# Full row gathers without a bounds check, and the last expert weights loaded in eight pieces

## The reference

```python
top_val, top_idx = lax.top_k(logits, TOP_K)          # 4 of 32 experts for each of 512 tokens
gate = jax.nn.softmax(top_val, axis=-1)
...
def expert_block(args):                              # 1024 -> 2048 -> 1024, all float32
    xb, e = args
    hc = xb @ w1[e] + b1[e]
    glu = jnp.minimum(hc[..., :D_FF], SWIGLU_LIMIT)
    lin = jnp.clip(hc[..., D_FF:], -SWIGLU_LIMIT, SWIGLU_LIMIT)
    act = glu * jax.nn.sigmoid(SWIGLU_ALPHA * glu) * (lin + 1.0)
    return act @ w2[e] + b2[e]
...
y_assign = yrows[row] * sorted_gate[:, None]
out = jax.ops.segment_sum(y_assign, sorted_tok, num_segments=T)
```

## Time and profile before

| | us |
|---|---|
| median of 3 runs (1811.76 to 1812.91) | 1812.0 |
| the profiled execution | 1812.0 |
| its span, first to last instruction | 1810.3 |
| PE busy | 1712.9 |
| DVE / ACT / POOL busy | 451.7 / 385.9 / 105.0 |

### The profile page before, as it was taken

The page is one execution under the profiler, slowest core; times in us unless marked ns, Lnnn a source line. Parts: engine busy times, 40 slices in busy tenths (PEclk is TensorE's granted clock), DMA queues, the critical chain, the costliest instruction groups (busy, mean ns, idle before and its releaser), DMA issues.

```text
span 1810.3 us, 36236 instructions
## 1 busy us (share of the span) xinstructions
PE 1712.9 (95%) x15650; PEld 948.9 (52%) x15650; DVE 451.7 (25%) x847; ACT 385.9 (21%) x602; POOL 105.0 (6%) x186
## 2 busy tenths in 40 slices
PE   7999999999999998999999999999999999898986
PEld 5766687888788766434344343334333333343332
DVE  4354425424635345711010101000000000010005
ACT  5464233333335325000000000001000000000001
POOL 0010000000000010000000000000000000000013
PEclk9999999999999999999999999999999999999998
DMA  7202231224226333999999999999999999999986
GB/s 238 70 24 82 77 97 59 70 93 163 91 72 202 124 89 124 361 388 384 399 410 398 410 398 410 397 411 398 410 410 398 408 410 402 410 407 404 412 342 223
DMA packets 105712, 501.17 MB, mean 277 GB/s; under 512 B 11628, under 2 KB 22396, under 8 KB 56320
## 3 DMA queue, kind: packets, MB, share of 16 engines
q1 hardware_dynamic: 83904, 461.40, 64.7%
q0 software_dynamic: 8352, 24.44, 4.3%
q10 hardware_dynamic: 13312, 13.12, 2.1%
HBM read 488.28 MB, written 15.20 MB: 278 GB/s over the span
## 4 chain that ended last, share of the span: by engine, by line
PE 61%; SPq 22%; DMA 9%; DVE 3%; issue 3%; ACT 2%; ACTq 0%; POOL 0%; DVEq 0%
SPq L487 22%; PE ps L1903 15%; PE ps L1583 9%; PE ps L1584 9%; PE ps L1585 9%; PE ps L1927 7%; DMA ring<-in_w_exp_in 7%; DMA moe<-in_w_exp_in 2%; PE ps L1680 1%; PE ps L1735 1%; PE ps L1754 1%; PE ps L469 1%; PE ps L1971 1%; DMA raw<-in_w_in 1%; PE ps L1624 1%
## 5 line engine op out<-in xcount | busy, mean ns | idle before, releaser
L1903 PE MATMUL ps<-ring,moe 128*32 128x512 f32 x4408 | 489.9, 594 | 22.8 <-DMA ring<-in_w_exp_in 22.6
L1903 PEld LDWEIGHTS ps<-ring,moe 128*32 128x32 f32 x4408 | 130.9, 110 | 364.9 <-issue 269.5
L1483 DVE TENSOR_SCALAR moe<-ps 128x768 f32<-128x768 f32 (+1 forms) x32 | 28.0, 874 | 880.3 <-PE ps L1903 880.3
L1927 PE MATMUL ps<-ring,moe 128*32 128x256 f32 x4320 | 239.8, 379 | 3.8 <-DMA ring<-in_w_exp_out 3.8
L1055 DVE TENSOR_TENSOR wl<-raw,wh 128x1024 fp32r<-128x1024 f32 x104 | 126.3, 1224 | 259.1 <-ACT wh L716 259.1
L1927 PEld LDWEIGHTS ps<-ring,moe 128*32 128x32 f32 x4320 | 129.0, 110 | 104.4 <-DMA ring<-in_w_exp_out 7.4
L716 ACT ACTIVATE wh<-raw 128x1024 fp32r<-128x1024 f32 x104 | 108.9, 1057 | 255.5 <-PE ps L1585 254.9
L1583 PE MATMUL ps<-oph,wh 128*128 128x512 f32 x384 | 151.4, 394 | 2.4 <-DVE work L1188 1.6
L956 ACT ACTIVATE moe<-ps 128x768 f32<-128x768 f32 (+1 forms) x32 | 23.8, 744 | 594.2 <-DVE moe L1483 594.2
L1584 PE MATMUL ps<-opl,wh 128*128 128x512 f32 x384 | 150.0, 391 | 0.0
L1585 PE MATMUL ps<-oph,wl 128*128 128x512 f32 x384 | 149.7, 390 | 0.0
(11 more groups left out here) (305 smaller groups left out, 1536.6 us busy)
## 6 DMA issues: line engine op xcount, KB each, us to landing
ring<-in_w_exp_in SPq DMA_DIRECT2D x205, 1024.0 KB, 28.0
ring<-in_w_exp_out SPq DMA_DIRECT2D x104, 1024.0 KB, 29.3
moe<-in_w_exp_in SPq DMA_DIRECT2D x51, 1024.0 KB, 28.5
raw<-in_w_in SPq DMA_DIRECT2D x26, 1024.0 KB, 5.1
moe<-in_w_exp_out SPq DMA_DIRECT2D x24, 1024.0 KB, 28.9
raw<-in_w_ckv SPq DMA_DIRECT2D x8, 1024.0 KB, 5.1
y_main<-moe ACTq DMA_DIRECT2D x84, 96.0 KB
raw<-in_w_ret_o SPq DMA_DIRECT2D x4, 1024.0 KB, 4.9
```

What stands on the lines that cost most here:

```text
L1483: nc.vector.tensor_scalar(act_n[:, 0:g], ps[:, 0:g, 256:512].rearrange("p j (n a) -> p j a n", a=2), 1.0 - LIMIT, 1.0 + LIMIT, ALU.max, AL ...
L1903: ins = nc.tensor.matmul(ps[32 * s:32 * s + 32, j, :], xt[:, k, 32 * j:32 * j + 32], w[:, s, :, :], start=False, stop=(k == KT - 1), tile_ ...
L1927: ins = nc.tensor.matmul(y_bank(s, j), at[:, a, j, q, :], w[:, a, s, :], start=False, stop=(q == W2 - 1 and a == 1), tile_position=(0, 32 ...
```

## The change

It has three parts.

1. *Gathers.* The bounds check goes from `gather_rows` and `late_row`. The table of token numbers is no longer shifted, so a pad's index is 0 and the DMA reads row 0 of `h_rows` for it; for `y_late` a DVE `max` with 0 makes the index of a token that has no row there 0 too. All rows of a gather are now moved.
2. *What the first part makes needless.* The clearing of `xrows` on POOL with its semaphore `zero_x`, one of two DVE instructions for `rowl`, and the addition in `index`, which becomes a copy.
3. *The last chunk.* The one DMA of 128 rows becomes eight, of 2, 4, 6, 8, 10, 12, 14 and 72 rows of 8 KB, each of the first seven with a semaphore of its own. PE waits for all eight ahead of the last quarter of `last_down`.

```diff
-    tok[:, :, 0] = P * np.arange(TT)[None, :] - 2 * T
+    tok[:, :, 0] = P * np.arange(TT)[None, :]
...
             sp.wait_ge(w_used, DP + CHUNKS - SLOTS)
-            load(final, EC - 1, (CHUNKS - 1) % SLOTS)
+            row = 0
+            for n, landed in zip((2, 4, 6, 8, 10, 12, 14), w_edge):
+                rows = slice(row, row + n)
+                sp.dma_start(held((CHUNKS - 1) % SLOTS)[rows, :], expert_chunk(final, EC - 1)[rows, :]).then_inc(landed, 16)
+                row += n
+            rows = slice(row, P)
+            sp.dma_start(held((CHUNKS - 1) % SLOTS)[rows, :], expert_chunk(final, EC - 1)[rows, :]).then_inc(w_ring[(CHUNKS - 1) % SLOTS], 16)
...
                 pool.indirect_dma_start(out=xrows[0:32 * g, :], out_offset=None, in_=h_rows,
-                                        in_offset=bass.IndirectOffsetOnAxis(ap=idx[0:32 * g, :], axis=0),
-                                        bounds_check=T - 1, oob_is_err=False).then_inc(x_in, 16)
+                                        in_offset=bass.IndirectOffsetOnAxis(ap=idx[0:32 * g, :], axis=0)).then_inc(x_in, 16)
...
             pool.wait_ge(xt_made, 1)
-            nc.gpsimd.memset(xrows, 0.0).then_inc(zero_x, 1)
             pool.wait_ge(idx_out, 1)
-            pool.wait_ge(zero_x, 1)
             gather_rows(groups(1))
...
                 pool.indirect_dma_start(out=late[t], out_offset=None, in_=y_late,
-                                        in_offset=bass.IndirectOffsetOnAxis(ap=rowl[:, t:t + 1], axis=0),
-                                        bounds_check=CAP - 1, oob_is_err=False).then_inc(late_in[t], 16)
+                                        in_offset=bass.IndirectOffsetOnAxis(ap=rowl[:, t:t + 1], axis=0)).then_inc(late_in[t], 16)
...
-                nc.vector.tensor_scalar(idx[0:32 * g, :], ps[0:32 * g, 3, 0:1], float(2 * T), None, ALU.add).then_inc(idx_out, 1)
+                nc.vector.tensor_copy(idx[0:32 * g, :], ps[0:32 * g, 3, 0:1]).then_inc(idx_out, 1)
...
-            chain(nc.vector.tensor_scalar(tmp_l[:, 0:TT], names["rlate"], float(LATE_ROW), 8192.0, ALU.is_lt, ALU.mult))
-            chain.wait()
-            chain(nc.vector.scalar_tensor_tensor(rowl, names["rlate"], float(-LATE_ROW), tmp_l[:, 0:TT], ALU.add, ALU.add))
+            chain(nc.vector.tensor_scalar(rowl, names["rlate"], float(-LATE_ROW), 0.0, ALU.add, ALU.max))
...
                 for q in range(W2):
+                    if q == W2 - 1:
+                        for edge in w_edge:
+                            pe.wait_ge(edge, 16)
                     w = chunk_in(down_chunk(NE - 1, q)).rearrange("p (a h n) -> p a h n", a=2, h=2)
```

More of the change, by code:

```diff
@@ L361, in layer_kernel @@
         w_ring = [sem(f"w_ring{n}") for n in range(SLOTS)]
+        w_edge = [sem(f"w_edge{n}") for n in range(7)]
         w_hi, w_lo, w_used = sem("w_hi"), sem("w_lo"), sem("w_used")
@@ L398, in layer_kernel @@
         last_used, diag_ready = sem("last_used"), sem("diag_ready")
-        zero_x = sem("zero_x")
         pickl_ready, gl_made, gl_kept, last_done = (sem(n) for n in ("pickl_ready", "gl_made", "gl_kept", "last_done"))
```

## The result

The changed kernel takes 1823.1 us (median of 4 runs, 1822.68 to 1826.49), the kernel before 1811.88 us beside it: a ratio of 1.0067, 95% interval 1.0053 to 1.0082. Twelve more executions took 1821.2 to 1829.9 us. It is slower by 9.6 to 14.9 us. I had forecast 1813.0 us, in a range up to 1823; the result lies at its upper edge and just outside, on the side to which I gave a chance of 0.31.

A forecast was written before the change was run, and what follows sets the result against it. The prediction held that weight loads on all 16 DMA engines set the pace for most of the experts. It summed 1812.0 + 1.0 + 0 + 0 + 0 = 1813.0 us, own range 1811 to 1815.5, over the cases 1806 to 1823.

The forecast's parts named there:

- Gathers of the experts: Expert stage: pads add 2.60 MB of moved rows; cost taken as 1 us, between ends of 0 and 14.0.
- The upper end: Expert stage: pads as dear as gathers of real rows, 5.9 MB at 420 GB/s, 14.0 us.
- The reading of the earlier trace: End of the weight stream: share 0.35 at 1751 us, so ten or more engines are done, about 19 us ahead.
- What becomes needless: Start of the expert stage: dropped memset of 0.95 us and DVE instruction of 0.17 us are hidden; 0 us.
- Late gathers: Four `y_late` gathers at the end: each grows by 0.46 MB, 1.1 us, within 3.9 to 5 us of slack; cost 0.
- The last chunk: Eight issues instead of one ahead of the last quarter of `last_down`: slow issues and semaphores cost nothing; 0 us.
- The slack of 3.3 to 7.7 us: Last quarter of `last_down`: the last chunk lands by 1770 to 1774.4 us, PE wants it at 1777.7.
- the tail gets slower: Rival: late gathers of mostly one row, or eight slowly issued pieces, eat the slack; 3 to 5 us, chance 0.07.
- dear pads: Rival in the expert stage: pads cost like other traffic, 5.2 to 14.0 us, 1817.2 to 1826.0 us; chance 0.26.
- The idle 9.06 us shrink: Rival ahead of `last_down`: dividing the last chunk otherwise shortens PE's idle stretch, 1803 to 1809.5 us; chance 0.18.
- POOL's 10.49 MB: Sign in the profile after: POOL's queue moves 10.5 MB between 755 and 1719 us, against 7.89 MB before.
- the stream of weights: Sign of being wrong, at the end of the expert stage: the weights' stream ends later by 5 us or more.

The follow-up runs named there:

- e3_experts: Kernel before with only the experts' 31 gathers reading full rows (no bounds check, shift or clearing); late gathers and last chunk unchanged: ratio 1.0015, 1812.83 us.
- e12_skipped: Kernel before with token numbers shifted so the bounds check skips every row of the experts' gathers; experts compute on zeros: ratio 0.9746.
- e4_late: Kernel before with only the four gathers of `y_late` reading full rows: ratio 1.0010, 1812.47 us.
- e1_gathers: Kernel before with all gathers reading full rows, no bounds check, the last chunk still in one load: ratio 1.0017, 1812.68 us.
- e5_even: Kernel before with the last chunk in eight pieces of 16 rows each, gathers keeping their bounds check: ratio 1.0026.
- e2_pieces: Kernel before with only the last chunk changed, into eight pieces of 2 to 14 and 72 rows; gathers keep their check: ratio 1.0032, 1815.38 us.
- e9_far: Kernel before with the last chunk in eight pieces of 16 rows, each taking rows 8 apart in memory and in partitions: ratio 1.0025.
- e10_read_near: Kernel before with the last chunk in eight 16-row pieces, reading neighbouring rows, writing partitions 8 apart (other weights multiplied): 1816.48 us, one run.

## Why the prediction was wrong

*Gathers of the experts.* Right in kind and nearly in size. I took 1 us between ends of 0 and 14.0; e3_experts measured 2.7 us (1.1 to 4.2). Most pads fall on engines that are ahead, as the landings of the last chunk show (three engines lose their lead, the last landing is 1.4 us later). The upper end worked from the earlier trace rows played no part. The equal shares that I worked with (8 rows of a chunk, 6 or 4 rows of a gather for an engine) fit the semaphores: in the kernel before that of a weight chunk rises in 16 steps (128 / 16), and that of the 31 gathers in 496, 16 for each (96 / 16 or 64 / 16). The reading of the earlier trace rows, five or six engines busy of 16, was the right one to weigh most. The sentence beside it, that only gathers load engines unevenly, was half true (e12_skipped), and it did no harm because the lead was read from the trace and not built from it.

*What becomes needless.* 0, as forecast: the first gather starts at 736.4 us against 736.0.

*Late gathers.* The step "each grows by 0.46 MB, 1.1 us at 420 GB/s" failed: the landing grew by 3.8 us, from 3.8 to 7.6. I had priced the bytes and left out that these gathers run beside the early ones, which move 128 rows each; that this is the reason is likely and not shown. (The remark that a landing four times as long would cost 3 to 8 us was too low as well: 4 x 3.8 us from 1779.99 is 6.4 us past 1788.84.) The slack was smaller too. I read it off one execution in which PE idles 9.06 us ahead of `last_down`. In the changed kernel it idles 7.25 there, 10.58 in e12_skipped, and 0.9 in each of the other eleven traces, in the same place of the same stream. ACT has it too. Its copy of what `down` of turn 30 made (first line: before, second: e4_late) starts 6.9 us behind the end that the profile has for `down` (1761.34 us) in the kernel before, and 0.1 us behind it (1763.87) in e4_late:

```profile
1768.20 0.38 ACT L969 ACTIVATE moe<-ps 128x256 f32<-128x256 f32 x1 [16.36 <-remote]
...
1763.95 0.38 ACT L968 ACTIVATE moe<-ps 128x256 f32<-128x256 f32 x1 [9.59 <-PE ps L1924]
```

It waits for PE's count `w_used`, which rose at 1768.17 us, and for stores that had landed by 1743.6. So the stretch lies ahead of that count and not in `last_down`; what holds PE there is open. Without that idle time the late gathers are on the path: PE waits 3.44 us for one in e4_late. Alone they cost 1.8 us (0.4 to 3.4).

*The last chunk.* This is the term that failed: "I take 0, since the slow issues come from a queue that is full of weights, which is no longer so after 1751 us." SP's issues were near the quick end of what I said (1745.8 to about 1752 us), and no cost of the eight semaphores is to be seen. That slow issues come from a full queue was my reading of one trace: in the kernel before an issue of line 487 takes 333 ns in the median from 738 to 1000 us (1138 at most), and 1.9 to 2.8 us, by the tile, from 1500 us on, where PE waits for weights. Of the seven issues of line 528 in the changed kernel one takes 2277 ns and another 1071, and the other five 258 to 319 ns, all by about 1751 us, so the cause is not shown. But I had priced only the issue and the landing of the pieces themselves, at the speed of one large load, and only for one who waits for them, PE ahead of its last quarter. In fact the weight packets in flight beside them take 0.54 instead of 0.31 us for nine microseconds (0.78 with 16 rows each). That delays the last `down` chunk of turn 30, for which POOL's gathers at the end wait, and with them the late gathers and the products behind. Measured 5.8 us (3.8 to 7.8). This path through POOL is nowhere in my sum. The slack of 3.3 to 7.7 us was none for PE, since in e1_gathers, with one load, PE already waits 2.14 us for the last chunk; but it was not the slack that counted either.

On the size of pieces the runs say that those of 128 KB, in e5_even (1.0026), were about as bad as those of 16 to 112 KB with one of 576 KB behind them (1.0032, e2_pieces). The intervals are 0.001 to either side, so what the uneven division costs by itself can't be told. In the trace of e2_pieces, behind a first step at its issue, the semaphore of each piece of 2, 4, 6, 8, 10, 12 and 14 rows rises in 2, 4, 6, 8, 10, 12 and 14 further steps, and that of the 72 rows in 12; I read these steps as the number of engines that had a share.

*The sum.* 1812 + 2.7 + 1.8 + 5.8 is 1822.3 us with what the parts measured alone (1820.9 with e1_gathers for both kinds of gathers); the change measured 1823.1. Of the rivals, "the tail gets slower" (chance 0.07) had named both failing terms, late gathers and pieces, and gave them 3 to 5 us; they took more, and by another path than slow issues. That the changed kernel came out at the upper end of the range over the cases is luck: that end stood for dear pads. *The idle 9.06 us shrink* found no support in the pieces: 0.9 us stand there with one load too (e1_gathers, e3_experts, e4_late), and 7.25 with eight pieces. The kernel before has one trace, so how often it idles there is not known.

Of the signs that I had named, POOL's 10.49 MB and PE's 93.80 us came as forecast. `last_down` started 7.0 us later (1777.97 against 1771.00), the products waited for `y_late`, and the stream of weights ended some 17 us later (the last share landed at 1786.9 us against 1769.7), which I had given as a sign of being wrong.

## What to carry to other kernels

A slack read off a single execution is worth no more than the idle time in front of it: look whether that idle time has a releaser, and if it has none, price the step as if it weren't there. A load that is cut into pieces must be priced by what it does to the loads in flight beside it (here 0.54 instead of 0.31 us for a packet of 8 KB), and for all who wait for those, not only by its own landing. Before trusting the waits of one engine, read the chain that ended last: here it ran through POOL. Spreading the real rows of a gather over all partitions gained 6.9 us here, more than all the pads cost (2.7 us).

## What the runs showed of the hardware

- Eight loads of 16 rows x 8 KB, one after another, where one load of 128 rows stood: a packet of 8 KB takes 0.78 us instead of 0.31 while they are worked through (e5_even); 0.60 to 0.64 when the partitions of a piece are 8 apart (e9_far, e10_read_near). Whether its rows in memory are near or far makes no difference to this (0.60 and 0.64, 0.78 and 0.78).
- Leaving out the real rows of the experts' gathers gains 46 us for 18.8 us of bytes (e12_skipped); adding pad rows, most of them on engines that were ahead, costs 2.7 us for 6.2 (e3_experts).
- The semaphore of a load from SP of 2, 4, 6, 8, 10, 12 or 14 rows rises, behind a first step at its issue, in as many steps as it has rows, that of one of 72 rows in 12 (e2_pieces), that of one of 16 rows in 16 (e5_even). Read as shares of engines, a short load is on as many engines as it has steps.
- With `bounds_check` a gather leaves out the rows whose index lies past it: 2560 rows of 4 KB are 10.49 MB without the check and 7.89 MB with it (755 to 1719 us, after and before), and 0.01 MB where all lie past it (e12_skipped). The packets are 3040 each time.
- With nothing gathered, eight of 16 engines still have their last weights 15 us or more before the other eight (1710.2 against 1725.2 us, share 0.51 to 0.60 from 1708 us on, in e12_skipped).
- Ahead of `last_down` PE idles 7 to 11 us in three traces (before 9.06, after 7.25, e12_skipped 10.58) and 0.9 us in the eleven others. The cause is open.
